# One projection of a hybrid decoder layer in two parts, and a square root moved ahead of three PSUM copies

## The reference, cut to what matters

```python
h = rms_norm(x, attn_norm_g[l])
u = h @ w_in[l]
(u_q, u_kc, u_vc, u_ks, u_vs, u_kw, u_vw, u_gate, u_qkv, u_z, u_a, u_b) = jnp.split(u, splits, axis=-1)
...
q = rms_norm(u_q.reshape(B, T, G, HPG, DH), q_norm_g) * (DH ** -0.5)      # group A
ss = jnp.einsum('bghqd,bgqnsd->bghqns', qb, ksel)...                      # scores
ps = masked_probs(ss, smask)
...
qkv = jax.nn.silu(causal_dwconv(u_qkv, conv_w))                           # group B
```

## Time and profile before

| | |
|---|---|
| median of 3 runs | 1149.26 us (1148.83 to 1150.24) |
| profiled execution | 1148.68 us, of which the span is 1146.7 us |
| PE busy | 1090.6 us, 95% of the span |
| DVE, ACT, POOL busy | 343.2, 198.0, 34.4 us |
| DMA | 429.87 MB, 374 GB/s read over the span |
| mean granted TensorE clock | 0.994 of full speed |

### The profile page before, as it was taken

One profiled execution on the slowest core, in us unless ns is written; L12 is line 12 of the kernel. 1 busy time (PEld: TensorE's weight loads), 2 busy tenths in 40 slices (PEclk: granted clock), 3 DMA queues, 4 the chain that ended last, 5 costly groups with the idle time before them and its releaser, 6 DMA issues.

```text
span 1146.7 us, 12560 instructions
## 1 busy us (share of the span) xinstructions
PE 1090.6 (95%) x5163; PEld 452.5 (39%) x5163; DVE 343.2 (30%) x693; ACT 198.0 (17%) x389; POOL 34.4 (3%) x45
## 2 busy tenths in 40 slices
PE   8999999999999999999899999989899999999996
PEld 5577587543333333333233333333333333333332
DVE  2477745322231313222222231313122213222222
ACT  4246754310000000101010100000001000101000
POOL 1001240000000000000000000000000000000000
PEclk9999999999999999999999999999999999999999
DMA  9824234799999999999999999999999999999994
GB/s 318 273 74 128 93 148 167 299 417 429 433 428 433 429 430 432 433 426 434 430 430 432 429 435 428 432 432 429 432 432 432 430 432 432 430 430 430 433 423 162
DMA packets 34791, 429.87 MB, mean 375 GB/s; under 512 B 6380, under 2 KB 11980, under 8 KB 20652
## 3 DMA queue, kind: packets, MB, share of 16 engines
q1 hardware_dynamic: 34732, 429.02, 89.3%
HBM read 427.96 MB, written 1.05 MB: 374 GB/s over the span
## 4 chain that ended last, share of the span: by engine, by line
PE 70%; DMA 22%; DVE 3%; ACT 3%; issue 1%; SPq 0%; POOL 0%; DVEq 0%; ACTq 0%; POOLq 0%
PE bank L1043 44%; DMA ring<-in_exp_w_up_dram 14%; DMA nsa<-in_exp_w_up_dram 7%; PE bank L629 4%; PE bank L616 4%; PE bank L1084 3%; PE bank L646 3%; PE bank L887 2%; ACT nsa L1128 2%; PE bank L982 2%; PE bank L1014 2%; DVE nsa L1896 1%; PE bank L637 1%; PE bank L1072 1%; DVE nsa L1892 1%
## 5 line engine op out<-in xcount | busy, mean ns | idle before, releaser
L1043 PE MATMUL bank<-ring,nsa 128*64 128x512 f32 x2464 | 543.3, 595 | 17.4 <-DMA ring<-in_exp_w_up_dram 9.2
L1043 PEld LDWEIGHTS bank<-ring,nsa 128*64 128x64 f32 x2464 | 174.8, 137 | 367.0 <-issue 343.2
L1128 ACT ACTIVATE nsa<-bank 128x512 f32<-128x512 f32 (+7 forms) x153 | 77.9, 528 | 511.3 <-PE bank L1014 250.3
L1043 PE MATMUL bank<-nsa 128*64 128x512 f32 x608 | 136.3, 601 | 4.5 <-DMA nsa<-in_exp_w_up_dram 3.1
L1886 DVE TENSOR_SCALAR nsa<-bank 128x512 f32<-128x512 f32 x32 | 22.1, 691 | 227.2 <-PE bank L1043 227.2
L1902 DVE COPY nsa<-bank 64x512 f32<-64x512 f32 x32 | 22.2, 694 | 213.1 <-PE bank L1043 213.1
L1125 ACT ACTIVATE nsa<-nsa 128x512 f32<-128x512 f32 (+3 forms) x36 | 21.3, 594 | 339.8 <-DVE nsa L1886 339.7
L1043 PEld LDWEIGHTS bank<-nsa 128*64 128x64 f32 x608 | 42.8, 138 | 92.7 <-issue 84.7
L1892 DVE TENSOR_SCALAR nsa<-bank 128x512 f32<-128x512 f32 x32 | 22.1, 691 | 168.9 <-PE bank L1043 168.9
L1084 PE MATMUL bank<-nsa 128*128 128x512 f32 x128 | 59.5, 604 | 12.5 <-ACT nsa L1128 12.5
L1014 PE MATMUL bank<-rA,nsa 128*64 128x512 f32 x264 | 62.3, 592 | 0.1
(11 more groups left out here) (215 smaller groups left out, 631.5 us busy)
## 6 DMA issues: line engine op xcount, KB each, us to landing
ring<-in_exp_w_gate_dram SPq DMA_DIRECT2D x22, 4096.0 KB, 35.5
ring<-in_exp_w_up_dram SPq DMA_DIRECT2D x22, 4096.0 KB, 37.6
ring<-in_exp_w_down_dram SPq DMA_DIRECT2D x21, 4096.0 KB, 35.0
nsa<-in_exp_w_down_dram SPq DMA_DIRECT2D x6, 4096.0 KB, 34.9
nsa<-in_exp_w_up_dram SPq DMA_DIRECT2D x5, 4096.0 KB, 33.6
nsa<-in_exp_w_gate_dram SPq DMA_DIRECT2D x5, 4096.0 KB, 37.8
ring<-in_exp_w_down_dram SPq DMA_DIRECT2D x9, 2048.0 KB, 12.7
ring<-in_exp_w_gate_dram SPq DMA_DIRECT2D x8, 2048.0 KB, 11.9
```

The lines of the kernel that those rows point to most:

```text
L1043: i = pe.matmul(o[64 * fh:64 * fh + 64, :], lt, wc, start=(opens and cc == 0), stop=(cc == 7), skip_group_check=True)
L1128: return nc.scalar.activation(o, i, ACT.Copy)
```

## The change

Three edits. In PE's program, the first half (`u` = 0) of `qkv(3)`, which is `PROJ[0]`, is put between the transposes of tile 0's keys and step 0, and the second half stays where the whole was, behind the scores of step 0. The bank list follows: `PROJ[0]` takes its bank ahead of the two score jobs of step 0. In ACT's program, the square root of the second tile goes ahead of the copies of `QKV[0]`, qT and kT.

```diff
-    j += [...] + [("qkv", QKV[0]), ("qT", 0), ("kT", 0)]
+    j += [...] + [("qkv", QKV[0]), ("qT", 0), ("kT", 0), PROJ[0]]
...
-        if i < len(PROJ):
+        if 0 < i < len(PROJ):
             j += [PROJ[i]]
...
-            def qkv(i):
+            def qkv(i, parts=(0, 1)):
 
                 s, val, _ = slab[f"q{i // 2}"]
                 w = ringv(s).rearrange("p (c n) -> p c n", c=KC)
                 pe.wait_ge(landed[s], val)
-                o = take(("qkv", i))
-                for u in range(2):
+                o = take(("qkv", i)) if parts[0] == 0 else ps[bank["qkv", i][0]]
+                for u in parts:
                     mc0 = (2 * i + u) % 4 * P
                     for c in range(KC):
                         m = pe.matmul(o[:, u * SEQ:(u + 1) * SEQ], w[:, c, mc0:mc0 + P], hT[:, c, :],
                                       start=(c == 0), stop=(c == KC - 1))
-                done(m, ("qkv", i))
+                if parts[-1] == 1:
+                    done(m, ("qkv", i))
...
             turn_nsa(0)
+
+            qkv(PROJ[0][1], parts=(0,))
             for i, (t, b, g) in enumerate(steps):
...
-                        qkv(j)
+                        qkv(j, parts=(1,) if i == 0 else (0, 1))
...
             act.wait_ge(sem("cin_zeroed"), 1)
+            root(ssn[:, 1, :], "ssn_ready", "sqn_ready", 2)
             ev_qkv(QKV[0])
             ev_nsa(0)
-            root(ssn[:, 1, :], "ssn_ready", "sqn_ready", 2)
```

More of the change, by code:

```diff
@@ L134, in pe_front_order @@
     j += [("uc", 1)] + [("ub", t) for t in range(T2)] + [("vecT",)]
-    j += [("ua", 0), ("gc",), ("gb", 0), ("gb", 1), ("ua", 1)] + [("qkv", QKV[0]), ("qT", 0), ("kT", 0)]
+    j += [("ua", 0), ("gc",), ("gb", 0), ("gb", 1), ("ua", 1)] + [("qkv", QKV[0]), ("qT", 0), ("kT", 0), PROJ[0]]
     for i, (t, b, g) in enumerate(attn_steps()):
```

## The result

The changed kernel takes 1147.85 us (median of 20 runs, 1146.42 to 1149.68), the kernel before 1149.30 us (median of 20). One run of the kernel before took 6456.79 us; it is no part of the ratio, and without it the median is 1149.26 us. The gain is 1.45 us by the medians, 0.13%. The ratio over the runs is 0.9984 with a 95% interval of 0.9978 to 0.9990, so 0.16% or 1.8 us, with 1.1 to 2.5 us as its bounds. The forecast was 1147.9 us. The profiled execution is 1147.61 us, its span 1145.6 us.

The account below looks back on a forecast made before the run. PE bounds 70% of the chain, DMA 22%; near 60 us PE's wait with its clock drop and DVE's wait overlap. Median 1149.26 minus 1.4 (0.65 sure, half of 1.55) gives 1147.9 us, range 1146.4 to 1149.5.

Parts of the forecast that it names:

- Two waits over each other: Near 60 us, PE's wait and slow clock cost 3.98 us; DVE's late weights stop PE's gain alone at 1.6 us.
- The root: ACT issues tile 1's square root 0.03 us behind the mean square; DVE free at 59.38 instead of 62.43, copies not delayed.
- The first half and the scores: PE runs 3.46 us of qkv(3) over ACT's copies; DVE starts on the scores at 61.78, its step taking 6.34 us.
- The sum: PE starts PROJ[1] at 68.60 instead of 70.80 after a new 1.75 us wait: 2.20 us gained against the profile.
- the fall: Clock at 1.2 GHz behind PE's 2.05 us wait, about 60.29 to 63.70; costs the kernel before 1.55 us.
- the fall moves: Rival: the lower clock follows PE's new wait before the weights' transposes; 1.3 us slower, 1150.5 us, chance 0.06.
- The share of the runs with a fall: The lower clock near 60 us was taken for half the kernel before's runs: 0.65 + 1.55 / 2 = 1.4 us.
- Does the gain reach the end: PE's releases in the front start the experts' DMA stream, so the whole rest shifts earlier by PE's gain.
- Full gain: Rival: lower clock near 60 us in most runs before, never after; 2.20 us gained, 1147.1 us, chance 0.27.
- Only DVE's gain: Rival: lower clock near 60 us rare, in the profile by chance; 0.65 us gained, 1148.6 us, chance 0.18.
- A bank or a copy in the way: Rival: PROJ[0]'s copy waits for the square root, or PROJ[1] for its bank; at most 0.6 us, failing cover 0.04.

Follow-up runs that it names:

- the split: Changed kernel with the square root left behind the copies, so only PE's edits against the kernel before: 1148.14 us, ratio 0.9991.
- idle matmuls: Kernel before plus four matmuls with unused results in PE's wait: 1148.06 us; with ACT's square root also moved ahead of the copies: 1148.11 us.
- the quarter: Changed kernel with 4 instead of 8 of the 16 matmuls of qkv(3) ahead of the scores: 1146.13 us, ratio 0.9976 to the kernel before.
- the second profile: Kernel before, unchanged, profiled once more; the clock stayed up behind the 2.05 us wait: 1150.55 us.
- the root alone: Kernel before with only ACT's edit, the second tile's square root ahead of the copies: 1149.53 us, ratio 1.0002.

## Why the prediction was right, step by step

**Two waits over each other: right.** Each cover alone is worth one part: the root 0 (13.64), the split 1.31 (12.38), both 1.98 (11.71). The root's part shows only where the clock stays up: 12.38 to 11.71 with the split, 12.38 to 11.95 with idle matmuls.

**The root: right.** ACT starts it at 56.99, 0.10 us behind the mean square (56.72 + 0.17), where the prediction had 0.03; the reciprocal follows 0.10 us behind, and no copy is delayed (57.37, 0.04 behind `QKV[0]`'s end). The table load lies beneath the wait for the scores.

**The first half and the scores: right.** 3.46 us; DVE's start 61.98 against 61.78, of which 0.22 is the later start of this execution. DVE's step takes 68.33 - 61.98 = 6.35 us (its last instruction, at 67.64, is 0.69 us long by the timeline) against 6.34, so ACT's copies and the load of L461 beside it cost it nothing. The new wait was given as 1.75 and is 1.76 us.

**The sum: 2.20 forecast, 1.98 measured.** The term that was off is the four transposes behind the wait: 0.66 instead of 0.44 us. The row of 0.44 in the earlier trace rows had no wait ahead of it; at the full clock they take 0.66 behind a wait, here and in the profiles of the split, the idle matmuls and the quarter. Since a kernel before without the fall waits there too (0.15 us in the second profile), it has the 0.66 as well, and the gain against it is 12.37 - 11.71 = 0.66 us (0.65 forecast, since the missing 0.22 us stood on both sides of that difference). The fall thus costs 1.32 us and not 1.55.

A second term was too high. The prediction took all of 1.58 - 0.86 = 0.72 us of the scores for the fall. But behind the wait they take 1.10 us at the full clock as well (the second profile of before), so the fall costs PE 1.58 - 1.10 + 8.12 - 6.91 = 1.69 us and not 1.93. This didn't touch the forecast, since the weights of DVE set the start of `PROJ[1]` in that case; it is why PE stands for them 0.15 us and not 0.38, and the rival "the fall moves" took its price of 1.93 us from the same sum. Of the 1.69 us, 1.32 reach the start of `PROJ[1]`; without the fall the other 0.37 go into the wait for DVE (0.15) and the slower transposes behind it (0.22).

**The share of the runs with a fall.** I took one half; four profiles of the kernel before show three, and the root alone, which has nearly the same wait (2.00 us), shows one more; behind the wait of 2.44 us in the split alone it didn't come. With three of four the gain would be 0.66 + 0.75 * 1.32 = 1.65 us, with one half 1.32; the medians say 1.45, the ratio 1.8 and its interval 1.1 to 2.5. The runs don't settle the share more closely than this. That the forecast of 1147.9 us met the median of 1147.85 so closely is thus partly luck: a share that was probably too low and a price of the fall that was too high cancel in part, and the medians and the ratio differ by 0.4 us between themselves. The Trainium skill (TensorE: Matmul & The Clock Gate, Part 1) states that the monitor behind the clock is free-running and isn't reset when a kernel starts, so that the same kernel can meet it differently from run to run. The traces agree in that the same program has the fall in one execution and not in the next: 13.69, 12.37, 13.69 and 13.70 us. That this is the cause, no run here shows.

**Does the gain reach the end: right.** 1.96 us at the first experts' matmuls; beyond that only the timed runs speak, and their interval of 1.1 to 2.5 us holds it.

**The rivals.** "Full gain" is the kernel with the fall in all runs, 1.98 us as measured; it holds for three of the four profiles, and the timed runs don't exclude it. "Only DVE's gain" is the second profile; as the gain of all runs, 0.66 us lies outside the interval. "The fall moves" didn't come: no fall behind the new wait in two profiles, and filling it gains nothing. That a fall never comes there isn't shown by that. "A bank or a copy in the way" didn't come either. What the prediction didn't see is that half of the projection is too much: it had noted DVE's wait of 2.4 us for the scores and didn't follow it to a better split. Nor did it count PE's wait of 3.12 us ahead of 565.15, which has a fall behind it too.

## What to carry to other kernels

When an engine's wait lies on the chain, look for a second one beneath it that ends just later, and price both: alone, the root was worth nothing and the split 1.3 us, and together they were worth 2.0. Filler put ahead of work that another engine waits for should end when the wait does and not later: against a profile with the fall, 1.73 us of it gave 3.2 us by the distance, 3.46 gave 2.0, and 6.91 lost 4 to the end of `PROJ[1]`. These are three sizes at one place of one kernel; nothing between them was tried. Where a short wait of PE is followed by a lower clock in some executions, one profile prices it wrongly; take several, or fill the wait with matmuls that nobody reads, which tells the clock's price by itself.

## What the runs showed of the hardware

Four transposes of 128x128 take 0.44 us in a stream of PE's work and 0.66 us behind a wait for DVE, however short it is (0.15 us before them in the second profile of before). Four records of the scores (128x256) take 0.86 us in a stream and 1.10 us behind a wait, at the full clock in both cases.

The same wait of 2.05 us on PE was followed by the lower clock (1.2 GHz) for about 3.4 us in three of four executions of one program. Around the wait of 5.21 us the clock was at the lower level for about 6.8 us. The length of a wait alone decides neither whether there is a fall nor how long it lasts. The same place of the experts' stage (L982, L985 after the change) shows it in three executions:

```profile
565.15 1.74 PE L982 MATMUL bank<-btab,nsa 32*64 32x512 f32 x8 [3.12 <-issue]
563.02 1.98 PE L985 MATMUL bank<-btab,nsa 32*64 32x512 f32 x8 [2.72 <-issue]
562.76 1.09 PE L985 MATMUL bank<-btab,nsa 32*64 32x512 f32 x8 [2.94 <-issue]
```

The first is the kernel before, with the clock low for 3.4 us (565.5 to 568.9); the second the profile after, low for 6.8 us (562.5 to 569.3); the third the second profile after, which stays at 1.00.
